# The opening of the expert stage: banks given out anew, first scores and token rows behind two half chunks

## The reference

```python
q = (hc @ w_pq).reshape(PEER_CHUNK, PEER_HEADS, 2, PEER_DK_HALF)
sc = jnp.einsum('thcd,chnd->thcn', q, sub_keys)
vals, idx = lax.top_k(sc, PEER_TOPK)
cand = vals[:, :, 0, :, None] + vals[:, :, 1, None, :]
cand_idx = idx[:, :, 0, :, None] * N_KEYS + idx[:, :, 1, None, :]
top_s, top_c = lax.top_k(cand.reshape(..., TOPK * TOPK), PEER_TOPK)
experts = jnp.take_along_axis(cand_idx.reshape(...), top_c, axis=-1)
g = jax.nn.softmax(top_s, axis=-1)
ue, ve = peer_u[experts], peer_v[experts]
act = gelu(einsum('td,thkd->thk', hc, ue))
return einsum('thk,thkd->td', g * act, ve)
```

## Time and profile before

| | |
|---|---|
| median of 3 runs | 1853.44 us |
| the profiled execution's own time | 1849.03 us |
| its span, first to last instruction | 1847.1 us |
| mean granted TensorE clock | 0.965 |
| PE, DVE, ACT, POOL busy | 84%, 62%, 40%, 13% |
| the 256 gathers | issued from 560.3 to 1209.9 us, the last dot starts at 1223.2 us |

### The profile page before, as it was taken

One profiled execution on the slowest core, in us unless ns is written; L12 is line 12 of the kernel. 1 busy time (PEld: TensorE's weight loads), 2 busy tenths in 40 slices (PEclk: granted clock), 3 DMA queues, 4 the chain that ended last, 5 costly groups with the idle time before them and its releaser, 6 DMA issues.

```text
span 1847.1 us, 20636 instructions
## 1 busy us (share of the span) xinstructions
PE 1546.8 (84%) x7910; PEld 1153.6 (62%) x7910; DVE 1150.0 (62%) x2004; ACT 736.0 (40%) x1333; POOL 248.4 (13%) x271
## 2 busy tenths in 40 slices
PE   7798988799888777777777777767899998789998
PEld 6688977798687223222332222236699878569987
DVE  5248778864557666766676676447654558854354
ACT  4244564424333333333333333333445335444532
POOL 0000000000002333333333333310000000000000
PEclk9899999899999999999999999988999999999999
DMA  5663335254248999999999999942155553114563
GB/s 216 160 227 137 141 134 183 75 185 151 91 160 312 423 421 422 422 421 422 421 412 422 422 415 411 423 193 91 69 182 180 186 182 121 46 69 174 182 192 114
DMA packets 71746, 443.66 MB, mean 240 GB/s; under 512 B 6975, under 2 KB 9279, under 8 KB 26208
## 3 DMA queue, kind: packets, MB, share of 16 engines
q0 software_dynamic: 36864, 268.45, 35.1%
q1 hardware_dynamic: 29888, 163.59, 25.6%
q10 hardware_dynamic: 4896, 10.31, 2.1%
HBM read 439.17 MB, written 3.15 MB: 239 GB/s over the span
## 4 chain that ended last, share of the span: by engine, by line
PE 51%; DMA 25%; DVE 15%; ACT 5%; issue 3%; ACTq 0%; POOL 0%; DVEq 0%
PE banks L906 23%; DMA arena<-experts,xn 22%; PE banks L935 15%; PE banks L1172 8%; DVE w_lo L1297 3%; DMA scratch<-arena 2%; DVE arena L1713 2%; DVE arena L1579 1%; PE banks L1039 1%; PE banks L1026 1%; ACT w_hi L520 1%; ACT xn L778 1%; DVE xn L1385 1%; DVE arena L1857 1%; ACT xn L782 1%
## 5 line engine op out<-in xcount | busy, mean ns | idle before, releaser
L1172 PE MATMUL banks<-arena,xn 128*128 128x512 f32 x1024 | 478.4, 612 | 157.8 <-ACT xn L782 156.3
L1297 DVE TENSOR_TENSOR w_lo<-raw,w_hi 128x2048 fp32r<-128x2048 f32 x154 | 352.1, 2290 | 294.8 <-PE banks L906 126.2
L1172 PEld LDWEIGHTS banks<-arena,xn 128*128 128x128 f32 x1024 | 187.1, 192 | 448.8 <-ACT xn L782 256.0
L1713 DVE CUSTOM_DVE_ANT_0 arena<-arena,banks 128x1024 f32<-128x1024 f32 x256 | 312.3, 1220 | 213.4 <-DMA arena<-experts,xn 210.9
L520 ACT ACTIVATE w_hi<-raw 128x2048 fp32r<-128x2048 f32 x154 | 292.9, 1907 | 209.3 <-PE banks L935 125.6
L495 POOL DMA_INDIRECT arena<-experts,xn x256 | 241.1, 942 | 452.2 <-PE banks L1172 384.9
L906 PE MATMUL banks<-op_hi,w_hi 128*128 128x256 f32 x1520 | 229.1, 292 | 18.0 <-ACT op_hi L579 10.5
L906 PE MATMUL banks<-op_hi,w_lo 128*128 128x256 f32 x1520 | 219.9, 289 | 19.7 <-DVE w_lo L1297 19.7
L906 PEld LDWEIGHTS banks<-op_hi,w_hi 128*128 128x128 f32 x1520 | 203.2, 196 | 28.1 <-issue 18.0
L906 PE MATMUL banks<-op_lo,w_hi 128*128 128x256 f32 x1520 | 217.1, 286 | 0.0
L906 PEld LDWEIGHTS banks<-op_hi,w_lo 128*128 128x128 f32 x1520 | 201.2, 197 | 22.0 <-DVE w_lo L1297 22.0
(11 more groups left out here) (214 smaller groups left out, 1193.3 us busy)
## 6 DMA issues: line engine op xcount, KB each, us to landing
raw<-wstream SPq DMA_DIRECT2D x154, 1024.0 KB, 4.9
arena<-experts,xn POOLq DMA_INDIRECT x256, 13.3
scratch<-arena ACTq DMA_DIRECT2D x1, 2048.0 KB
arena<-scratch ACTq DMA_DIRECT2D x2, 1024.0 KB, 8.7
xn<-mem_in ACTq DMA_DIRECT2D x2, 1024.0 KB, 4.8
x<-x_in SPq DMA_DIRECT2D x1, 1024.0 KB, 5.8
arena<-keys_in ACTq DMA_DIRECT2D x1, 1024.0 KB, 5.1
out_dram<-x SPq DMA_DIRECT2D x1, 1024.0 KB, 4.0
```

Of the source, the lines that this page charges most:

```text
L1172: mm = pe.matmul(sums[:, n, :], diag[:, s, :], rows[:, s, D + n * CW:D + (n + 1) * CW], start=False, stop=False, skip_group_check=True)
L1297: dve.tensor_tensor(w_lo[:, n % LO, :, :], raw[:, n % RAW, :, :], w_hi[:, n % HI, :, :].bitcast(F32), ALU.subtract).then_inc(lo_ready, 1)
L1713: dve.tensor_tensor_reduce(u, u, token_rows[k // PAIRS][:, :, :], 1.0, 0.0, ALU.mult, ALU.add, dots[:, s:s + 1]).then_inc(dot_ready, 1)
```

## The change

- `plan()` gives banks by an explicit count for each bank. All products keep their banks but `pq`, which now takes only banks 0 and 1 in turn; all other results keep theirs but the scores, which take only banks 4 and 5 in turn.
- Token rows of block 0 go to banks 2 and 3 as before, those of block 1 to banks 0 and 1 (before 4 and 5); row sums of block 0 to banks 6 and 7 (before 0 and 1), of block 1 to banks 4 and 5 (before 6 and 7).
- PE's order is now: pq 0 and 1, token rows of block 0, scores (0,0), pq 2, 3, 4, scores (0,1), pq 5, 6, scores (0,2), pq 7, scores (0,3) and (1,0) to (1,3). The 3 slots are given free once these are made (without the wait for their copies), and token rows of block 1 stand between the row sums of k = 32 and k = 33.
- ACT copies scores (0,1) behind pq 4 and (0,2) behind pq 6, and gives `gelu_ready` at the start of the stage. The `high_parts` call beside `top_exps` asks for what `copy_lin` has just made.
- DVE makes low parts ahead of the first selection only up to pq 2 (before: pq 4). The selection of head 0 makes those of pq 3, 4 and 5, that of head 1 those of pq 6, pq 7 and the first of the next weight, `ina` 0. The low part of `ina` 1 follows the 16 dots of head 0. DVE waits for scores (0,j) only before the selection that needs them.

```diff
+    def place(where, uses, key, bank=None):
+        bank = len(where) % 4 if bank is None else bank
+        where[key] = 4 * uses[bank] + bank
+        uses[bank] += 1
...
-            lin.setdefault(key, len(lin))
+            place(lin, lin_uses, key, len(lin) % 2 if c == "pq" else None)
...
-        misc[name] = len(misc)
+        place(misc, misc_uses, name, len(misc) % 2 if name[0] == "sc" else None)
...
-        token_rows = bank_pairs[1], bank_pairs[2]
-        row_sums = bank_pairs[0], bank_pairs[3]
+        token_rows = bank_pairs[1], bank_pairs[0]
+        row_sums = bank_pairs[3], bank_pairs[2]
...
+            act.sem_inc(gelu_ready, 1)
             for j in range(8):
                 copy_lin(("pq", j), q_peer[:, 2 * j:2 * j + 2, :])
                 if j == 1:
                     copy_scores(0, 0)
-
+                if j in (4, 6):
+                    copy_scores(0, j // 2 - 1)
                 if j in (3, 5):
+                    high_parts(LAST["pq", j] + 2)
                     top_exps(0, (j - 3) // 2)
-            for tb in range(TB):
-                for j in range(4):
-                    if tb or j:
-                        copy_scores(tb, j)
-            act.sem_inc(gelu_ready, 1)
+            copy_scores(0, 3)
+            for j in range(4):
+                copy_scores(1, j)
...
+            features(1, **normed("ffn"))
             token_rows_of(0)
-            for tb in range(TB):
-                for j in range(4):
-                    if tb or j:
-                        scores_of_keys(tb, j)
+            for j in range(2):
+                lin_emptied(pe, ("pq", j))
+            pe.wait_ge(keys_in_s, 16)
+            pe.sem_inc(row_free, EARLY_SLOTS)
+            scores_of_keys(0, 0)
+            for n in range(2, 8):
+                half_chunk(True, 1)
+                if n in (4, 6):
+                    for j in (n - 2, n - 1):
+                        lin_emptied(pe, ("pq", j))
+                    scores_of_keys(0, n // 2 - 1)
+            for j in (6, 7):
+                lin_emptied(pe, ("pq", j))
+            scores_of_keys(0, 3)
             for j in range(4):
-                misc_emptied(pe, ("sc", TB - 1, j))
+                scores_of_keys(1, j)
+            wait_misc(pe, ("sc", 1, 3))
             pe.wait_ge(peer_zero, 1)
             pe.sem_inc(row_free, GSLOTS - EARLY_SLOTS)
-            token_rows_of(1)
...
                     mm.then_inc(row_free, 1)
+                    if k == 2 * TOPK:
+                        token_rows_of(1)
...
-                        low_parts(min(halves[0] + 1, upto if steps[0] < 13 else upto + 2))
+                        low_parts(min(halves[0] + 1, upto))
...
-            low_parts(LAST[("pq", 3)] + 1)
+            low_parts(LAST[("pq", 1)] + 1)
             misc_emptied(dve, ("sc", 0, 0))
             for h in range(AHEAD):
-                top_experts(0, h, None, LAST[("pq", 2 * h + 3)] + 2)
-            low_parts(LAST[("pq", 7)] + 2)
-            for j in range(1, 4):
-                misc_emptied(dve, ("sc", 0, j))
+                top_experts(0, h, None, LAST[("pq", 5 + 2 * h)] + h)
+            low_parts(LAST[("pq", 7)])
...
+                if n == 0:
+                    low_parts(LAST[("pq", 7)] + 2)
```

More of the change, by code:

```diff
@@ L95, in plan @@
     lin, last, misc, early = {}, {}, {}, {}
+    lin_uses, misc_uses = [0] * 4, [0] * 4
+    def place(where, uses, key, bank=None):
+        bank = len(where) % 4 if bank is None else bank
+        where[key] = 4 * uses[bank] + bank
+        uses[bank] += 1
     half = wide = 0
@@ L101, in plan @@
             if FIRST_CHUNK[norm_] == n:
-                lin["roots", norm_] = len(lin)
+                place(lin, lin_uses, ("roots", norm_))
         i = seen.get(c, 0)
@@ L111, in plan @@
             for j in range(2):
-                lin.setdefault((c, 2 * i + j), len(lin))
+                if (c, 2 * i + j) not in lin:
+                    place(lin, lin_uses, (c, 2 * i + j))
                 last[c, 2 * i + j] = half
@@ L368, in chain @@
             eng.wait_ge(s, count[id(s)])
-        token_rows = bank_pairs[1], bank_pairs[2]
-        row_sums = bank_pairs[0], bank_pairs[3]
+        token_rows = bank_pairs[1], bank_pairs[0]
+        row_sums = bank_pairs[3], bank_pairs[2]
+        MISC_ORDER = {key: n for n, key in enumerate(MISC)}
         def lin_bank(key):
@@ L385, in wait_misc @@
         def wait_misc(eng, key):
-            eng.wait_ge(misc_full, MISC[key] + 1)
+            eng.wait_ge(misc_full, MISC_ORDER[key] + 1)
         def empty_lin(ins, key):
@@ L861, in fill_misc @@
             def fill_misc(key):
-                assert MISC[key] == state["misc"], key
+                assert MISC_ORDER[key] == state["misc"], key
                 state["misc"] += 1
@@ L1128, in scores_of_keys @@
                 mm.then_inc(misc_full, 1)
[L1131 to L1141, removed]
             def token_rows_of(tb):
@@ L1150, in token_rows_of @@
                 mm.then_inc(hf_ready, 1)
+            features(1, **normed("ffn"))
             token_rows_of(0)
-            for tb in range(TB):
-                for j in range(4):
-                    if tb or j:
-                        scores_of_keys(tb, j)
+            for j in range(2):
[12 more added lines that the diff above has]
+            scores_of_keys(0, 3)
             for j in range(4):
-                misc_emptied(pe, ("sc", TB - 1, j))
+                scores_of_keys(1, j)
+            wait_misc(pe, ("sc", 1, 3))
             pe.wait_ge(peer_zero, 1)
             pe.sem_inc(row_free, GSLOTS - EARLY_SLOTS)
-            token_rows_of(1)
             for tb in range(TB):
                 sums = row_sums[tb]
+                if tb:
+                    for j in range(4):
+                        misc_emptied(pe, ("sc", tb, j))
                 for n in range(2):
@@ L1739, in _ @@
                 m = n + AHEAD
-                if m == PH:
-                    for j in range(4):
-                        misc_emptied(dve, ("sc", 1, j))
+                if m < TB * PH and m % 2 == 0:
+                    misc_emptied(dve, ("sc", m // PH, m % PH // 2))
                 if m < TB * PH:
```

## The result

The kernel now takes 1840.7 us (median of 4 runs, 1838.95 to 1841.69); the kernel before, run beside it, took 1852.86 us (4 runs). The ratio is 0.9932, with a 95% interval of 0.992 to 0.9945: 0.7% faster, well beyond the 0.2% that can be told. The forecast was 1840.8. The profiled execution took 1841.69 us, with a span of 1839.9 (before: 1849.03 and 1847.1).

What follows compares the result with a forecast made beforehand. The prediction held the DMA to bound the stage while experts are gathered. Its terms, 13.2 + 1.9 - 2.5 - 0 = 12.6 us, taken from the median of 1853.44, gave 1840.8, with a range of 1835.5 to 1848.

Steps and rivals of the forecast that it cites:

- The gate: PE's signal that the 3 late slots are free: gather 5 goes at 571.6, 13.2 us earlier.
- The cover on DVE: Selections and low parts beside PE's chain keep ahead of it; the low part of pq 3 has 1.8 us to spare.
- the rival of a late low part: A low part late at pq 3 stalls PE; one stall costs 6.2 us, leaving 6.4; chance 0.14 (one stall or similar).
- the slower one: DVE falls behind and PE stalls at three of five half chunks: 6.0 us slower, 1859.4; chance 0.05.
- The cover on ACT: ACT's high parts and copies come in time; `ina` 1's raw load lands at 560, 4 us to spare before pq 7's copy.
- Gather 5 to gather 8: Opening of the gather stream: gather 8 follows by 4.9 us instead of 7.30, worth 1.9 us, ends 0 and 2.3.
- my two readings: Stream loss near gather 8 before the change: 1.2 us by GB/s in 595 to 600, or 2.3 by dot 8.
- The late load: The last raw load goes out near 605 into a full gather stream and costs 2.5 us; ends 0 and 2.5.
- Token rows between rows 32 and 33: Token rows of block 1 hold PE 3.64 us there, hidden by queued gathers: cost 0, other end 3.6.
- The sum: All terms together: 13.2 + 1.9 - 2.5 - 0 = 12.6 us gained, ends 7.1 and 15.5.
- The lock on GpSimd: Rule set aside: DVE copies could delay each of the first five gather issues; the trace showed 0.2 us at most.

Runs made afterwards that it cites:

- e4: Changed kernel with the token rows of block 1 put back ahead of the row sums, as before the change: 1839.81 us, ratio 0.9937.
- e1: Changed kernel with the low part of `ina` 1 made ahead of the dots, so its slot's raw load goes out earlier: 1838.95 us, ratio 0.9928.
- e2: Changed kernel with keys and queries swapped in memory, scores (1,0) and (1,1) behind pq 4, one more slot freed behind pq 5: 1838.07 us, ratio 0.992.
- e6: Changed kernel plus six two-input DVE subtractions of 128x2048, between dots later in the stage, into a tile nothing reads: 1842.25 us.
- e7: Changed kernel plus six one-input DVE copies of 128x2048, between dots later in the stage, into a tile nothing reads: 1840.51 us.
- e8: Changed kernel plus two one-input DVE copies of 128x2048, one behind the other, at each of six places between dots: 1840.13 us.

## Why the prediction was right

- **The gate.** Forecast 13.2 us for gather 5, at 571.6. Measured 571.21, in a trace in which the copy of pq 1 is 0.4 earlier too; from that copy it is 60.07 - 46.85 = 13.2. Scores (0,0) were copied by 529.5 (forecast 530.1), gather 0 came at 546.01 (546.7), PE's last five scores began at 565.84 (565.7). The sum of durations at full clock held to 0.1 us over 47, because no wait came in.
- **The cover on DVE.** I gave the low part of pq 3 1.8 us to spare. It ended at 531.59 + 2.28 = 533.87, and PE began to use it at 535.33: 1.5. No stall, so the rival of a late low part and the slower one fell with it.
- **The cover on ACT.** The raw load of `ina` 1 was forecast to land at 560 with 4 us to spare; it was issued at 550.4 and landed 9.9 us later, and ACT waited for it 0.24 us ahead of its high part at 560.37. The copy of pq 7 was due only at 565.14.
- **Gather 5 to gather 8.** Forecast 4.9 us, measured 5.22, before 7.30. The stream's part of this was mis-sized: I took 1.9 us from ends of 0 and 2.3, and e4 shows 1.1 by its bytes and 1.3 by its last dot. In the 16 us behind gather 5 the stream moved 5.60 MB, before 5.17, which at 421 GB/s is 1.0 us (in the repeats 5.63 and 5.31, 0.8 us). The lower of my two readings, 1.2 us lost by GB/s in 595 to 600, was the one to take. The wait ahead of dot 8 was no measure of it: from gather 5 to dot 8 the two profiles of before take 16.0 and 15.3 us, those of after 15.5 and 15.2.
- **The late load.** Forecast 2.5 us, with an issue near 605; issued at 609.80, worth 2.7 to 2.8 by e1.
- **Token rows between rows 32 and 33.** Forecast 0 of 3.6. On PE they last from 655.92 to 659.49, and POOL's timeline after shows gather 41 waiting 4.35 us for the row sums behind them, where e4 has 0.78:

```profile
656.36 0.94 POOL L505 DMA_INDIRECT arena<-experts,xn  x1 [2.59 <-PE banks L1185]
661.65 0.94 POOL L505 DMA_INDIRECT arena<-experts,xn  x1 [4.35 <-PE banks L1185]
```

The dots behind it go on at the stream's pace: from dot 40 to dot 60 after takes 49.8 us, its repeat 49.7, e4 50.6.

- **The sum.** Forecast 12.6. The last dot came 11.0 to 12.5 us earlier over the four pairs of profiles (mean 11.8), and the medians differ by 12.2 and 12.05. With the opening from gather 5 to gather 8 at 1.3 and the load at 2.7 the terms give 13.2 + 1.3 - 2.7 = 11.8. So the forecast was 0.8 high in its sum. That these terms meet the mean to 0.1 us is luck, as two profiles of before differ by 1.3; and that the forecast of 1840.8 lies 0.1 from the measured median is luck as well, since the median of before came out 0.6 lower (1852.86) than the 1853.44 that I started from. The forecast was made against an execution 4.4 us under its median and then put back on the median; the repeated profiles show that this was the right thing to do, as the difference lies behind the last dot. My low end of the range holds a slip: 1837.9 less 2 is 1835.9, not 1835.5. The 1836.4 that I gave for the profile's own time missed by 5.3: the profile of after had the long end.
- **The lock on GpSimd.** Here the argument was too weak. I set the rule of the Trainium skill (SBUF — State Buffer, SBUF: two separate sides), which as I gave it speaks of copies where a low part is a subtraction of two tiles, against 0.2 us beside a selection, and said that these gathers had lain beside a selection before. They had not lain beside a low part: before, the five issues run from 560.28 to 566.4, between low parts that end at 559.5 and start at 569.2. The change put one there, and gather 2 took 1.57 us longer to issue. It cost nothing, as the DMA still ran dry ahead of gather 5, and no term of the sum moved.

## What to carry to other kernels

A stage that is bound by its DMA is moved by what opens its stream or fills its holes, so add the durations of the chain from the last common instruction to the gate, and look at what must be ready beside it. Bytes that must be moved anyway belong into the stretch where the stream is dry, and once one hole is filled the next gate can take over, as gather 8 did in e2. So measure two such moves together, over the stretch in which they act, before you add their gains. When two profiles differ, compare from a common instruction to a common one, and set apart what lies behind it: here 6 us of chance sat in a part that nobody had touched.

## What the runs showed of the hardware

- A fp32 operation of DVE from SBUF to SBUF, 128x2048, holds up the issue of an indirect DMA on POOL that starts while it runs: 0.94 us becomes 1.81 to 2.69 beside a subtraction of two inputs (eight cases in after and e6), and 1.38 to 2.20 beside copies of one input (seven cases in e7 and e8). An issue that began 0.06 us behind the copy took 0.94, and so did one that began 0.21 us ahead of a low part (gather 4 of after, 552.77, low part at 552.98). The dots, which read one input from PSUM, lie beside such issues through the whole stage, whose mean stays 0.95 us. The Trainium skill (SBUF — State Buffer, SBUF: two separate sides) has the lock for copies; for the subtraction of two tiles in SBUF it was these runs that showed it.
- The same instructions behind the last dot took 623.2 to 629.7 us over twelve executions.
